# Seven weight buffers and one page queue for the block compression, and a merge chain that splits its operands one part at a time

## The reference, cut to what matters

```
# compressed branch of B: c = 0 keys, c = 1 values
blocks = cmp_full.reshape(B, n, 64, 2, KV, 128) + pe
hid = silu(einsum('bnlckd,cldf->bnckf', blocks, w1))   # w1: 2 x 64 x 128 x 128
kvc = einsum('bnckf,cfd->bnckd', hid, w2)
# merge of the two branches
mixed = (sig(gA) * (A @ w_oa) + sig(gB) * (B @ w_ob)) @ w_out
```

## Time and profile before

| | us |
|---|---|
| Median of three runs | 1898.4 (1898.15 to 1899.24) |
| Profiled execution, its own time | 1901.74 |
| Span of the profiled execution | 1900.3 |
| Compression, TensorE's first to last instruction | 839.75 to 971.47 |
| Merge, TensorE's first instruction to ScalarE's last tile | 1281.23 to 1433.54 |

### The profile page before, as it was taken

The page is one execution under the profiler, slowest core; times in us unless marked ns, Lnnn a source line. Parts: engine busy times, 40 slices in busy tenths (PEclk is TensorE's granted clock), DMA queues, the critical chain, the costliest instruction groups (busy, mean ns, idle before and its releaser), DMA issues. The chain is left out here.

```text
span 1900.3 us, 30126 instructions
## 1 busy us (share of the span) xinstructions
PE 1671.1 (88%) x11733; PEld 1475.2 (78%) x11733; DVE 744.7 (39%) x1290; ACT 550.4 (29%) x890; POOL 162.8 (9%) x177
## 2 busy tenths in 40 slices
PE   4899989999989979978679899889984999997996
PEld 2598989889889879857564454449984999997996
DVE  1244554543554522323424434443436333332223
ACT  3243333323333321210003323332133333341222
POOL 0012312312322301100000000000000000000000
PEclk9799999988999986987879999999997999998997
DMA  6422213112212142537433344344212333332211
GB/s 196 113 69 68 76 33 88 58 31 66 75 36 99 45 125 68 158 119 216 142 99 122 97 137 133 110 130 161 89 44 90 84 93 88 88 88 91 92 61 45
DMA packets 228784, 181.72 MB, mean 96 GB/s; under 512 B 8662, under 2 KB 221135, under 8 KB 228521
## 3 DMA queue, kind: packets, MB, share of 16 engines
q1 hardware_dynamic: 203530, 161.83, 28.3%
q10 hardware_dynamic: 25184, 18.96, 3.3%
HBM read 166.31 MB, written 23.02 MB: 100 GB/s over the span
## 5 line engine op out<-in xcount | busy, mean ns | idle before, releaser
L704 PE MATMUL dn_pg<-proj_xh,dn_wh 128*128 128x260 f32 x832 | 183.3, 296 | 6.9 <-DVE dn_wl L1003 6.4
L704 PE MATMUL dn_pg<-proj_xl,dn_wh 128*128 128x260 f32 x832 | 182.6, 296 | 0.0
L704 PE MATMUL dn_pg<-proj_xh,dn_wl 128*128 128x260 f32 x832 | 180.0, 294 | 0.0
L251 PE MATMUL gu_ps<-fh_xh,gu_wh 128*128 128x260 f32 x704 | 142.7, 284 | 19.0 <-DVE gu_wl L310 19.0
L251 PE MATMUL gu_ps<-fh_xh,gu_wl 128*128 128x260 f32 x704 | 142.8, 285 | 0.0
L251 PE MATMUL gu_ps<-fh_xl,gu_wh 128*128 128x260 f32 x704 | 142.6, 284 | 0.0
L704 PEld LDWEIGHTS dn_pg<-proj_xh,dn_wh 128*128 128x128 f32 x832 | 134.6, 195 | 8.6 <-DVE dn_wl L1003 7.9
L704 PEld LDWEIGHTS dn_pg<-proj_xh,dn_wl 128*128 128x128 f32 x832 | 134.9, 196 | 0.0
L704 PEld LDWEIGHTS dn_pg<-proj_xl,dn_wh 128*128 128x128 f32 x832 | 134.5, 195 | 0.0
L251 PEld LDWEIGHTS gu_ps<-fh_xh,gu_wh 128*128 128x128 f32 x704 | 109.6, 190 | 19.5 <-issue 19.5
L251 PEld LDWEIGHTS gu_ps<-fh_xh,gu_wl 128*128 128x128 f32 x704 | 109.5, 190 | 0.0
(11 more groups left out here) (472 smaller groups left out, 3356.6 us busy)
## 6 DMA issues: line engine op xcount, KB each, us to landing
all_ring<-in_w_gu SPq DMA_DIRECT2D x44, 512.0 KB, 5.0
all_ring<-in_w_in SPq DMA_DIRECT2D x32, 512.0 KB, 6.9
att_ada<-in_w_ada SPq DMA_DIRECT2D x16, 1024.0 KB, 5.3
fd_ring<-in_w_down SPq DMA_DIRECT2D x8, 1408.0 KB, 6.4
all_ring<-in_w_in SPq DMA_DIRECT2D x10, 1024.0 KB, 5.9
fr_ada<-in_w_ada SPq DMA_DIRECT2D x8, 1024.0 KB, 8.7
dn_xs<-in_w_in SPq DMA_DIRECT2D x16, 512.0 KB, 3.8
all_ring<-in_cmp_w ACTq DMA_DIRECT2D x16, 512.0 KB, 4.4
```

Of the source, the lines that this page charges most:

```text
L251: last = pe.matmul(self.ps[:, j, c, 0:HALF], w[:, j, k, :], x[:, k0 + k, c * HALF:(c + 1) * HALF], start=(k0 + k == 0 and w is self.wh and ...
L704: last = pe.matmul(pg[:, j, c, 0:HALF], w[:, j, k, :], x[:, k, c * HALF:(c + 1) * HALF], start=(k == 0 and term == 0), stop=(k == KD - 1 a ...
```

## The change

In the compression there are seven weight buffers. Five of them lie in a tile `late` whose first rows hold the bucket table `oh`; loads 2 to 6 wait until the "bias" units, which read that table, are done, and load n from 7 on waits for block n - 7. Loads 0 and 1 start the block on the ScalarE queue. All pages but (0, 2) and (0, 3) move to SP, and some of SP's stores move among them. The tails units move: one among the pages of c = 0, one behind the first eight blocks, one behind the third block of the second eight.

In the merge, tile 0's weights are split first. TensorE waits for part k just ahead of the products that use it, in the first of the four tiles of each loop step. B is split one part behind each tile of the first job, and `sg` one part behind each tile of the second, one tile late, with the last part where the third job begins.

```
     def run_products(self, pe):
-            if job.x:
-                pe.wait_ge(self.x_low, job.x + START)
...
                     for k in range(job.K):
+                        if job.source is not None and i == 0:
+                            pe.wait_ge(self.x_low, job.x - KD + k + 1 + START)
...
+    def steps(self, eng, job, ahead, empty, part):
+        follower = self.jobs[self.jobs.index(job) + 1:][:1]
+        if follower and follower[0].source is not None:
+            late = 1 if follower[0].source_steps else 0
+            for m in range(4 * job.iters):
+                ahead(job, m // 4, m % 4 + 1)
+                if empty:
+                    empty(eng, self, job, m // 4, m % 4)
+                if m >= late:
+                    part(follower[0], m - late)
+            return
...
+        def part(job, k):
+            if job.source_steps:
+                act.wait_ge(self.extra[1], k + 1 + START)
+            act.activation(job.pair[0][:, k], job.source[:, k], ACT.Copy).then_inc(self.x_high, 1)
         def split(job):
+            for k in range(KD - 1 if job.source_steps else 0, KD):
+                part(job, k)
...
-             ("page", 0, 2), ("page", 0, 3), ("bias", 0), ("bias", 1), ("page", 0, 4), ("page", 0, 5), ("page", 0, 6),
-             ("page", 0, 7),
+             ("page", 0, 2), ("page", 0, 3), ("bias", 0), ("bias", 1), ("page", 0, 4), ("page", 0, 5), ("tails", 0),
+             ("page", 0, 6), ("page", 0, 7),
...
-             ("page", 1, 0), ("page", 1, 1), ("tails", 0), ("page", 1, 2), ("page", 1, 3), ("tails", 1), ("page", 1, 4),
-             ("page", 1, 5), ("tails", 2), ("page", 1, 6), ("page", 1, 7)]
+             ("sample", 1), ("tails", 1),
+             ("page", 1, 0), ("page", 1, 1), ("page", 1, 2), ("page", 1, 3), ("page", 1, 4), ("page", 1, 5), ("page", 1, 6),
+             ("page", 1, 7), ("tails", 2)]
+    W = 7
...
+        late = ph.sb("late", [P, B_COLS])
+        oh = late[0:NBK, :]
+        w1 = [ring[:, n, 0:LC // 2, :].rearrange("p k (m f) -> p (k m) f", f=P) for n in range(2)]
+        w1 += [late[:, n * LC * P:(n + 1) * LC * P].rearrange("p (l f) -> p l f", f=P) for n in range(W - 2)]
...
             sp.dma_start(oh[:, 0:B_COLS], io["buckets"]).then_inc(tab_in, 16)
-            store_rows(0)
             load_page(sp, 0, 4)
             load_page(sp, 0, 5)
+            store_rows(0)
+            load_page(sp, 0, 6)
+            load_page(sp, 0, 7)
             store_rows(1)
...
+            for b in range(2):
+                load_page(sp, 1, b)
+            store_tails(0)
+            for b in range(2, 4):
+                load_page(sp, 1, b)
             store_rows(2)
             store_rows(3)
...
+            store_tails(1)
+            for b in range(4, NB):
+                load_page(sp, 1, b)
+            store_tails(2)
...
+            def load(n):
+                if n >= W:
+                    a.wait_ge(used, n - W + 1 + START)
+                elif n >= 2:
+                    a.wait_ge(turned, at["bias", 1] + 1 + START)
```

More of the change, by code:

```diff
@@ L261, in splits_before @@
         own = job.source is not None and (i == 0 or job.source_steps)
-        after = self.jobs[i + 1:i + 2]
-        return [job] if own else [], [j for j in after if j.source is not None and not j.source_steps]
-    def steps(self, eng, job, ahead, empty):
+        return [job] if own else []
+    def steps(self, eng, job, ahead, empty, part):
         last_job = job is self.jobs[-1]
+        follower = self.jobs[self.jobs.index(job) + 1:][:1]
[8 more added lines that the diff above has]
+            return
         with eng.Fori(0, job.iters - 1 if last_job else job.iters) as t:
@@ L287, in ahead @@
             act.activation(self.wh[:, j, 0:job.K], self.ring[:, b, 0:job.K, j * P:(j + 1) * P], ACT.Copy).then_inc(self.high, 1)
+        def part(job, k):
+            if job.source_steps:
+                act.wait_ge(self.extra[1], k + 1 + START)
+            act.activation(job.pair[0][:, k], job.source[:, k], ACT.Copy).then_inc(self.x_high, 1)
         def split(job):
[L290 to L293, removed]
+            for k in range(KD - 1 if job.source_steps else 0, KD):
+                part(job, k)
         for job in self.jobs:
-            own, after = self.splits_before(job)
-            for other in own:
-                split(other)
+            own = self.splits_before(job)
             if job is self.jobs[0]:
@@ L301, in run_high @@
                 act.activation(self.wh[:, 0, 0:job.K], self.ring[:, 0, 0:job.K, 0:P], ACT.Copy).then_inc(self.high, 1)
-            for other in after:
+            for other in own:
                 split(other)
-            self.steps(act, job, ahead, job.act)
+            self.steps(act, job, ahead, job.act, part)
     def run_low(self, v):
@@ L311, in low, with part @@
                             self.wh[:, j, 0:job.K].bitcast(F32), ALU.subtract).then_inc(self.low, 1)
+        def part(job, k):
+            v.wait_ge(self.x_high, job.x - KD + k + 1 + START)
+            v.tensor_tensor(job.pair[1][:, k], job.source[:, k], job.pair[0][:, k].bitcast(F32), ALU.subtract)\
+                .then_inc(self.x_low, 1)
         def split(job):
[L314 to L317, removed]
+            for k in range(KD - 1 if job.source_steps else 0, KD):
+                part(job, k)
         for job in self.jobs:
-            own, after = self.splits_before(job)
+            own = self.splits_before(job)
+            if job is self.jobs[0]:
+                low(job, 0, 0)
             for other in own:
                 split(other)
[L323 to L327, removed]
+            self.steps(v, job, low, job.dve, part)
 def square_sums(ph, st):
@@ L1157, in sparse_inputs @@
     units = [("rows", 0, 0), ("rows", 0, 1), ("page", 0, 0), ("page", 0, 1), ("rows", 1, 0), ("rows", 1, 1),
-             ("page", 0, 2), ("page", 0, 3), ("bias", 0), ("bias", 1), ("page", 0, 4), ("page", 0, 5), ("page", 0, 6),
-             ("page", 0, 7),
+             ("page", 0, 2), ("page", 0, 3), ("bias", 0), ("bias", 1), ("page", 0, 4), ("page", 0, 5), ("tails", 0),
+             ("page", 0, 6), ("page", 0, 7),
              ("rows", 2, 0), ("rows", 2, 1), ("slant", 0), ("slant", 1), ("rows", 3, 0), ("rows", 3, 1), ("sample", 0),
-             ("sample", 1),
-             ("page", 1, 0), ("page", 1, 1), ("tails", 0), ("page", 1, 2), ("page", 1, 3), ("tails", 1), ("page", 1, 4),
-             ("page", 1, 5), ("tails", 2), ("page", 1, 6), ("page", 1, 7)]
+             ("sample", 1), ("tails", 1),
+             ("page", 1, 0), ("page", 1, 1), ("page", 1, 2), ("page", 1, 3), ("page", 1, 4), ("page", 1, 5), ("page", 1, 6),
+             ("page", 1, 7), ("tails", 2)]
+    W = 7
     at = {u: n for n, u in enumerate(units)}
@@ L1174, in sparse_inputs @@
         cT = ph.sb("cT", [P, BLK, ROWS + 1])
-        w1 = ring[:, :, 0:LC // 2, :].rearrange("p s k (m f) -> p s (k m) f", f=P)
         hidden = ph.sb("hidden", [P, ROWS])
@@ L1178, in sparse_inputs @@
         rows = ph.sb("rows", [P, 2, 12 * P])
-        oh = ph.sb("oh", [NBK, B_COLS])
+        late = ph.sb("late", [P, B_COLS])
+        oh = late[0:NBK, :]
+        w1 = [ring[:, n, 0:LC // 2, :].rearrange("p k (m f) -> p (k m) f", f=P) for n in range(2)]
+        w1 += [late[:, n * LC * P:(n + 1) * LC * P].rearrange("p (l f) -> p l f", f=P) for n in range(W - 2)]
         rel = ph.sb("rel", [NBK, H])
@@ L1193, in sparse_inputs @@
         page_in = [ph.sem(f"page_in{i}") for i in range(4)]
-        w_in, row_out = ([ph.sem(f"{n}{i}") for i in range(2)] for n in ("w_in", "row_out"))
+        w_in = [ph.sem(f"w_in{i}") for i in range(W)]
+        row_out = [ph.sem(f"row_out{i}") for i in range(2)]
         block = ph.block()
@@ L1219, in _, with store_tails @@
             sp.dma_start(pe_rows, io["cmp_pe"][0]).then_inc(small_in, 16)
+            def store_tails(n):
+                sp.wait_ge(emptied, at["tails", n] + 1 + START)
+                part = slice(n * 1024, (n + 1) * 1024)
+                sp.dma_start(io["p_conv"].rearrange("a b j n -> (a b j) n")[:, part], tail_rows[0:3, :]).then_inc(tail_out, 16)
+                sp.dma_start(io["s_conv"][0, :, 2, part], tail_rows[3:11, :]).then_inc(tail_out, 16)
             sp.wait_ge(table_in, 16 + START)
@@ L1250, in _ @@
         def _(a):
[L1251 to L1256, removed]
+            def load(n):
[3 more added lines that the diff above has]
+                    a.wait_ge(turned, at["bias", 1] + 1 + START)
+                a.dma_start(w1[n % W], io["cmp_w1"][0, n // 8, n % 8 * LC:(n % 8 + 1) * LC].rearrange("l d f -> d l f"))\
+                    .then_inc(w_in[n % W], 16)
+            load(0)
+            load(1)
             a.wait_ge(table_in, 16 + START)
@@ L1260, in _ @@
             load_page(a, 0, 3)
-            load(0, 0)
-            load(0, 1)
             a.wait_ge(vec_ready, 1 + START)
             a.dma_start(vec_dram.ap(), vec).then_inc(vec_out, 16)
```

(17 more changed lines are left out.)

2 lines of the change are left out of this document (removed).

## The result

The changed kernel takes 1875.68 us (median of four runs, 1867.15 to 1879.61), the kernel before 1898.28 in the same company: a ratio of 0.9874, with a 95% interval of 0.984 to 0.9909 (the quotient of the two medians is 0.9881). The forecast was 1878, with a range of 1870 to 1886. The profiled execution took 1879.61, with a span of 1878.3.

What follows compares the result with a forecast made beforehand. TensorE, busy 88% of the span, was taken as the bound, so only its idle or half-clock time could come back: 13.5 us in the compression plus 7.0 in the merge, 20.5 off 1898.4, giving 1878, range 1870 to 1886.

Steps and rivals of the forecast that it cites:

- Step one: Compression up to block (0, 0): blocks start at 884.9 instead of 885.88, with two weight loads put earlier.
- The term for the page's company: Before block (0, 0): page (0, 1) lands 2.5 us sooner once loads and stores beside it move (0 to 3.3).
- Step two: Compression, first eight blocks: 26.0 us instead of 34.6, with weight loads hidden.
- Step three: Compression, page (1, 0) to block (1, 0): 25.5 us instead of 23.8, SP alone issuing sixteen page DMAs (22.8 to 28.1).
- Step four: Compression, second eight blocks: 20.1 us instead of 25.7, including a start at half clock of 2.1 (18.0 to 22.2).
- The merge: Merge as a whole: 7.0 us back net (3.3 to 8.9), from 9.5 back at tile 16 and 2.5 lost.
- The loss at tile 2: Merge, tile 2: 2.5 us lost, 0.6 by later data behind the gates and 1.9 by restarting at half clock.
- the 6.2: Merge, tile 2: the loss if the sooner `w_oa` load shares with the gates and delays them by 3.7 us.
- the late pages: Rival with late gates: slower page issue and landing, another slow block, gates late by 3.7; 8.4 us less, 1886; 14%.
- the weights: Rival, compression's first half: loads 2 to 6 meet pages and stores; 8.6 us less gain, 1886.5; 7%.
- the price per wait: Rival, merge: TensorE pays for each of 48 waits per part; from 0.43 us each they cost all 20.5; 5%.
- The clock: Rival: TensorE keeps the upper clock in step four, the last page and at tile 2; 4.9 us more, 1873; 12%.

Runs made afterwards that it cites:

- e2: The changed kernel's new merge with the compression of the kernel before: 1888.58 us, 0.9929 of the kernel before.
- e3: The changed kernel with weight loads 0 and 1 behind the bias table's transfers on the ScalarE queue: 1877.99 us, 0.9891 of the kernel before.
- e4: The changed kernel with pages (1, 6) and (1, 7) back on the ScalarE queue, between weight loads 14 and 15: 1871.32 us, 0.9816 of the kernel before.
- e1: The changed kernel's new compression with the merge of the kernel before: 1887.55 us, 0.9929 of the kernel before.
- e0: The changed kernel run again without any edit: 1877.43 us, 0.9852 of the kernel before.
- e5: The changed kernel with VectorE waiting for gate transfers singly at tiles 0 and 4, the other two at tile 7: 1871.71 us, 0.9826 of before.
- e7: The changed kernel with the wait per part in all four tiles of a loop step, 144 more waits: 1882.01 us, 0.9865 of the kernel before.
- e8: The changed kernel with four weight buffers instead of seven: 1881.08 us, 0.9881 of the kernel before.
- e9: The changed kernel with the edits of e3, e4 and e5 together: 1857.02 us, 0.977 of the kernel before.

## Why the prediction was right, point by point

**Step one was wrong**, in its sign: block (0, 0) 1.0 us sooner by the sum, 4.2 later in the profile. That profile is the worst of eight with those loads in front (47.4 to 50.4, mean 48.5); the old compression has 46.1 and, in e2, 47.5, so the means are 1.7 apart. The term for the page's company had something in it: from its last DMA to TensorE, page (0, 1) took 5.3 us before, 4.0 after, and 3.1 in e3. What failed was the half sentence that two weight loads go "earlier". I looked at what they leave, not at what they then stand before: 1 MB on the ScalarE queue ahead of the 128 bytes that every page waits for. With that undone (e3) the stretch is 45.2, where the step's forecast was 45.1, and not by luck: page (0, 1) is 2.2 us sooner (2.5 in the sum) and from there to block (0, 0) it takes 1.3 us more (1.5). In the first profile 1.2 us besides come from the way behind page (0, 1), where the 64 small bias products take 12.83 us (11.55 before, 11.3 to 13.3 over all profiles).

**Step two** was right in kind and 1.7 us too long (24.3 for 26.0): the units overlap the blocks by more than I took off. No weight was late.

**Step three** was right to 0.1 us, 25.6 for 25.5, and term by term: the first page left 3.1 us in (2.8), the last DMA 17.0 later (17.0), and TensorE saw it after 2.3 (2.5). e4 shows that the cause was the one named: the page issue took the place of the tails wait that the change removed. The step's lower bound, 22.8, doesn't come out of its own short values, which add up to 23.6.

**Step four** came out at 19.1 for 20.1, with one block at half clock as forecast. Over the profiles it is 18.4 to 20.0. The added semaphores show no cost: TensorE stands still for 0.82 us ahead of the attention before and after.

**The merge** gave 8.7 for 7.0. Tile 16 is the 9.5 of the sum. The loss at tile 2 was mis-sized: VectorE went on 18.1 us after ScalarE's first split, where the profile of before has 19.4. That is not the new merge's doing: e1, with the old one, has 18.1 too. Beside e1 the merge gave 8.2 us. Tile 2 is taken out 28.3 us after the first split in the changed kernel and 26.6 in e1, so the loss was 1.7 where I had 2.5. The `w_oa` load did leave sooner, 3.8 us after the gates' first issue (1270.40 for 1266.59) instead of 8.4, and the gates landed no later: at most 11.9 us after issue (13.1; 11.7 in e1, where that load leaves 8.3 us after them). That agrees with what the Trainium skill's page DMA: Bandwidth & Descriptors, Queues, rings and completion order, says of descriptors consumed in ring order, and speaks against the 6.2.

The errors of step one (-5.2) and of the rest (+4.3) nearly cancel, so the total, 19.5 for 20.5, is better than its parts. That is luck, and so is part of the nearness of 1875.68 to 1878: 2.5 of the 22.0 us between the two spans lie outside the changed code. The first profile is also the least favourable to the compression: where it runs unedited (after, e0, e1, e5 to e7) it lasts 116.5 to 119.4 us, 10.8 to 13.7 less than before, and the 13.5 of the sum lies in that. Of the rivals, the late pages fall by step three, the late gates by the landings, the weights by the first-half rows and e8, the price per wait by e7. The clock did not hold at any of the three places in the changed kernel; e4 shows that it can at block (1, 0). One bound was far off: whole times of this kernel scatter by more than the 0.2% that I gave as what a measurement can tell, and a few runs would not have shown a gain of 4 us.

## What to carry to other kernels

When a transfer is moved forward, look at what it now stands in front of: a megabyte on one queue holds up a few bytes on another, and a chain that begins with those bytes pays, here about 3 us. When a wait is removed, follow the next engine in program order to its next wait; here an early start ended at four transfers waited for together, and waiting for each where it is used gave 5.4 us. For streamed weights ask how far ahead a load must leave, not how many buffers fit.

## What the runs showed of the hardware

A tiny transfer is late when another queue's bulk runs. The table of relative biases, 1 KB, landed 5.0 us after issue with the two weight loads in front (4.6 to 5.2 over eight profiles), and after 1.5 in each of the four profiles without them in front (before, e2, e3, e9). The DMA engines in those microseconds of the changed kernel (us, busy (count) by engine, clock, DMA share, GB/s):

```profile
840.00:842.00 2.00, 0.77 (x4) 0.37 (x2) 0.00 (x0) 0.00 (x0) 0.00 (x0) 0.50 1.11 319
842.00:844.00 2.00, 0.00 (x0) 0.00 (x0) 0.00 (x0) 0.00 (x0) 0.00 (x0) 0.50 1.12 266
```

TensorE's clock can stay at the lower level through busy time. In the changed kernel's profile, in DeltaNet code that no edit touches, TensorE pauses 1.67 us before 451.26 and the granted clock is then at 0.50 until about 468, with the engine busy for 16.05 of these 16.74 us:

```profile
451.26 1.97 PE L774 MATMUL dn_A<-dn_e,dn_MT 128*128 128x64 f32 x8 [1.67 <-ACT dn_e L896]
```

```profile
448.00:456.00 8.00, 6.33 (x36) 6.13 (x36) 3.75 (x10) 3.43 (x6) 0.20 (x1) 0.69 0.25 66
456.00:464.00 8.00, 7.31 (x34) 6.91 (x34) 0.42 (x1) 1.93 (x4) 0.00 (x0) 0.50 0.00 0
464.00:472.00 8.00, 8.00 (x53) 8.00 (x53) 2.05 (x5) 2.07 (x3) 0.00 (x0) 0.74 0.04 4
```

In e3 the same instruction waits 1.68 us too (it starts at 453.65), and the 60 us from 420 on have a clock of 1.00, so the pause alone doesn't decide it. Stretches like this one come and go between executions of the same code, and between e3 and e7 the clock is what the difference upstream consists of. What decides it stays open.
